# Working the two tiles of a weight group side by side in the feed-forward input phases of a two-layer decoder kernel

## What is computed

```
def swiglu(x, w_in, w_out):
    gate, up = jnp.split(x @ w_in, 2, axis=-1)
    return (jax.nn.silu(gate) * up) @ w_out

h = x + 0.5 * rms_norm(swiglu(rms_norm(x, n_ffn1_pre), ffn1_w_in, ffn1_w_out), n_ffn1_post)
...
h = h + 0.5 * rms_norm(swiglu(rms_norm(h, n_ffn2_pre), ffn2_w_in, ffn2_w_out), n_ffn2_post)
```

## Time and profile before

| | |
|---|---|
| median of 3 runs | 1876.7 us (1876.03 to 1877.76) |
| span of the profiled execution | 1875.0 us, granted TensorE clock 0.993 |
| PE (TensorE matmul) busy | 1816.9 us, 97% |
| PEld (weight load) busy | 1758.3 us, 94% |
| DVE busy | 1342.1 us, 72% |
| ACT busy | 900.3 us, 48% |
| DMA | 368.2 MB, mean 196 GB/s |

### The profile page before, as it was taken

One profiled execution on the slowest core, in us unless ns is written; L12 is line 12 of the kernel. 1 busy time (PEld: TensorE's weight loads), 2 busy tenths in 40 slices (PEclk: granted clock), 3 DMA queues, 4 the chain that ended last, 5 costly groups with the idle time before them and its releaser, 6 DMA issues.

```text
span 1875.0 us, 40290 instructions
## 1 busy us (share of the span) xinstructions
PE 1816.9 (97%) x16206; PEld 1758.3 (94%) x16206; DVE 1342.1 (72%) x2083; ACT 900.3 (48%) x1045; POOL 118.9 (6%) x174
## 2 busy tenths in 40 slices
PE   6999999999999999999999999999999899979998
PEld 6999999988989999999999999998889799979998
DVE  6777577787777868776577766778776776877754
ACT  4443354546564354543354434465567445344433
POOL 0000001111210100000000000010111010000000
PEclk9999999999999999999999999999999999989999
DMA  7776656766764557565667766676777465546654
GB/s 229 207 211 192 178 186 222 239 225 219 270 218 148 188 180 224 160 180 163 182 194 217 204 180 189 201 244 207 231 237 250 160 210 163 177 116 182 182 166 125
DMA packets 433562, 368.20 MB, mean 196 GB/s; under 512 B 9394, under 2 KB 411060, under 8 KB 432754
## 3 DMA queue, kind: packets, MB, share of 16 engines
q1 hardware_dynamic: 409504, 276.60, 49.5%
q0 software_dynamic: 23872, 89.03, 14.1%
HBM read 338.90 MB, written 26.69 MB: 195 GB/s over the span
## 4 chain that ended last, share of the span: by engine, by line
PE 73%; DVE 13%; ACT 6%; issue 5%; DMA 2%; DVEq 0%; SPq 0%; ACTq 0%
PE proj L680 47%; PE proj L703 4%; PE proj L698 4%; PE proj L699 4%; DVE wl L1822 2%; PE proj L654 2%; ACT wh L1331 1%; PE aux L731 1%; PE aux L715 1%; PE aux L1120 1%; PE aux L1067 1%; PE aux L898 1%; DMA raw<-w_mem_v 1%; PE aux L843 1%; PE aux L859 1%
## 5 line engine op out<-in xcount | busy, mean ns | idle before, releaser
L1822 DVE TENSOR_TENSOR wl<-raw,wh 128x2048 fp32r<-128x2048 f32 (+1 forms) x280 | 599.2, 2140 | 199.7 <-ACT wh L1331 175.0
L1331 ACT CAST wh<-raw 128x2048 fp32r<-128x2048 f32 (+1 forms) x280 | 500.2, 1786 | 250.1 <-PE proj L680 106.4
L680 PE MATMUL proj<-xl,wh 128*128 128x264 f32 x2624 | 381.3, 286 | 1.3 <-DVEq L1965 1.3
L680 PE MATMUL proj<-xh,wh 128*128 128x264 f32 x2624 | 380.1, 288 | 0.0
L680 PE MATMUL proj<-xh,wl 128*128 128x264 f32 x2624 | 372.1, 284 | 2.2 <-DVE wl L1822 2.1
L680 PEld LDWEIGHTS proj<-xl,wh 128*128 128x128 f32 x2624 | 342.1, 189 | 14.6 <-issue 12.4
L680 PEld LDWEIGHTS proj<-xh,wl 128*128 128x128 f32 x2624 | 339.5, 189 | 4.0 <-DVE wl L1822 3.9
L680 PEld LDWEIGHTS proj<-xh,wh 128*128 128x128 f32 x2624 | 341.2, 189 | 2.2 <-issue 0.8
L699 PE MATMUL proj<-hl,wh 128*128 128x264 f32 x704 | 173.3, 283 | 0.0
L698 PE MATMUL proj<-hh,wh 128*128 128x264 f32 x704 | 173.0, 283 | 0.0
L1352 ACT ACTIVATE gate<-gate 128x264 f32<-128x264 f32 x88 | 37.4, 425 | 249.1 <-DVEq L1854 249.1
(11 more groups left out here) (465 smaller groups left out, 2283.7 us busy)
## 6 DMA issues: line engine op xcount, KB each, us to landing
raw<-ffn_w_in SPq DMA_DIRECT2D x176, 512.0 KB, 5.2
raw<-w_in SPq DMA_DIRECT2D x80, 1024.0 KB, 5.7
raw<-ffn_w_out SPq DMA_DIRECT2D x64, 704.0 KB, 4.6
sring<-cache_mem_k POOLq DMA_DIRECT2D x32, 512.0 KB, 5.2
sring<-cache_mem_v POOLq DMA_DIRECT2D x32, 512.0 KB, 4.3
out<-sring POOLq DMA_DIRECT2D x32, 512.0 KB, 4.3
sring<-state_gdn POOLq DMA_DIRECT2D x30, 512.0 KB, 5.9
raw<-w_mem_v SPq DMA_DIRECT2D x8, 1024.0 KB, 7.3
```

What stands on the lines that cost most here:

```text
L680: mm = pe.matmul(o, w[:, s, k * 256 + t * P:k * 256 + (t + 1) * P], a[:, k, :], **go)
L1331: act.copy(wh[:, slot, 0:size], raw[:, slot, 0:size]).then_inc(hi_done[slot], 1)
L1822: dve.tensor_sub(wl[:, slot, 0:size], raw[:, slot, 0:size], wh[:, slot, 0:size].bitcast(F32)).then_inc(split_done[slot], 1)
```

## The change

In the 21 groups of each `f1i` and `f2i` phase that are not written by hand, the two tiles are worked together: for each part, for each k-tile, one matmul of t = 0 and then one of t = 1. Both banks are waited for at the head of the group. All groups now have the order HIGH, INPUT_LOW, WEIGHT_LOW. `first_done` is raised by the last matmul but one of the group, `group_done` by the last.

```
-            def products(..., early=None, parts_of=None):
+            def products(..., early=None, parts_of=None, side_by_side=False):
...
+                    elif ph.tiles and side_by_side:
+                        for part in (HIGH, INPUT_LOW, WEIGHT_LOW):
+                            w, a = wl if part == WEIGHT_LOW else wh, low if part == INPUT_LOW else high
+                            if part == WEIGHT_LOW:
+                                pe.wait_ge(split_done[s], n + 2)
+                            for k in range(KT):
+                                for t in range(2):
+                                    bank = 2 * s + t
+                                    if part == HIGH and k == 0:
+                                        pe.wait_ge(bank_free[bank], bank_use(l, ph, i, u, bank) + 1)
+                                    mm = pe.matmul(proj[bank][:, 0:a.shape[2]], w[:, s, k * 256 + t * P:k * 256 + (t + 1) * P], a[:, k, :],
+                                                   start=(part == HIGH and k == 0), stop=(part == WEIGHT_LOW and k == KT - 1))
+                                    if part == WEIGHT_LOW and k == KT - 1:
+                                        mm.then_inc(group_done[s] if t else first_done, 1)
...
-                products(l, "f1i", xh, xl, early=halves(1), parts_of=unscaled(1))
+                products(l, "f1i", xh, xl, early=halves(1), parts_of=unscaled(1), side_by_side=True)
...
-                products(l, "f2i", xh, xl, early=halves(3), parts_of=unscaled(3))
+                products(l, "f2i", xh, xl, early=halves(3), parts_of=unscaled(3), side_by_side=True)
```

More of the change, by code:

```diff
@@ L631, in end, with products @@
                 mm.then_inc(aux_full[PLACE[name][0]], 1)
-            def products(l, name, high, low, kind="", after=None, branch=None, groups=None, mid=None, inner=None, early=None, parts_of=None):
+            def products(l, name, high, low, kind="", after=None, branch=None, groups=None, mid=None, inner=None, early=None, parts_of=None, side_by_side=False):
                 def group(ph, i, u):
```

## The result

The changed kernel takes 1881.69 us (median of 8 runs, 1880.93 to 1885.41) against 1877.23 us (8 runs) for the kernel before: a ratio of 1.0027, with a 95% interval of 1.0019 to 1.0036. It is slower by 4.5 us, and the forecast of 1877.6 us was 4.1 us too low. The profiled execution has a span of 1880.0 us, 5.0 over that of before. Further down, one of the ten runs of `p272_pad` took 9630.85 us where the other nine took 1878.09 to 1882.08; its time and ratio are those of the nine.

What follows compares the result with a forecast made beforehand. The prediction took TensorE's own matmul rate to bound the four input phases. Its terms, 0 + 1.0 - 0.2 + 0 + 0.1 = +0.9 us on 1876.7, gave 1877.6 us, with a range of 1873.5 to 1882.

Steps and rivals of the forecast that it cites:

- What bounds the kernel: Four input phases, 4032 matmuls in 487.6 us: TensorE's own rate sets their time, 120.8 ns per matmul.
- The operands' order: Input phases: new operand order costs 0 to +0.5 ns per matmul; half taken, +1.0 us.
- the operand order costs more: Rival for the input phases: 121.8 ns per matmul, +4.0 us, 1880.6 us in all; chance 0.13.
- The range: Whole kernel: 1873.5 to 1882 us, from pitch -1 to +1 ns per matmul plus smaller terms.
- The banks: Input phases: the 46 more bank changes per group cost or gain 0.
- the rival of a gain of up to 41.7 us: Input phases: alternating banks makes matmuls faster, up to 10.8 ns per bank change, giving 1835 us; chance 0.09.
- The waits for `wl`: Input groups: wait moves to matmul 33, so PE's two hold-ups in the third phase go, -0.2 us.
- The late gate: Input groups: gate and its consumers start about 1.15 us later, hidden by TensorE's work, cost 0.
- The rival of a late cast: Input groups: later loads and cast make PE wait for `wh`, 1881 us; chance 0.08.
- The head of the output phase: Layer 0's fifth output group: later cast makes PE wait 0 to 0.3 us once; +0.1 us taken.
- The sum: Whole kernel: 0 + 1.0 - 0.2 + 0 + 0.1 = +0.9 us, giving 1877.6 us.

Runs made afterwards that it cites:

- p272_pad: Kernel before with input tiles 272 columns apart in memory instead of 264; 1879.95 us, ratio 1.0013.
- e6_inputs_order: Kernel before with each input tile streamed twice in a row and the weight order kept, so wrong products; 1881.66 us, measured once.
- c_before_contig: Kernel before with the eight gate weight tiles contiguous in the slot, then the eight up tiles; 1877.38 us, ratio 1.0000.
- e1_one_bank: Changed kernel's operand order, but 24 matmuls in a row into one bank, sums mixed; 1882.5 us, ratio 1.0032.
- e2_banks_only: Operand order of the kernel before, but a bank change at every matmul, sums mixed; 1877.98 us, ratio 1.0002.
- e10_swept: Changed kernel, but all eight input tiles swept in order twice per part with alternating weight tiles, sums correct; 1876.83 us, ratio 1.0000.
- e4_late_signal: Kernel before with only the first tile's signal moved to the last matmul but one of the group; 1876.93 us, ratio 0.9999.
- e3_pair_apart: Changed kernel's side-by-side order and alternate banks, but each pair's second tile four k-tiles on, sums correct; 1882.38 us, ratio 1.0028.
- e7_one_tile_a: Kernel before, each input phase streaming one input tile throughout (tiles 0 to 3 by phase), wrong products; third phase 120.0 ns, then 121.0 ns per matmul.
- e5_weights_order: Weights in the changed kernel's order, inputs in the order of the kernel before, so wrong products; 1875.29 us, measured once.
- e11_base_16: Kernel before with `xh` moved by 16 bytes, `xl` by 48, what lies behind by 64; 1887.35 us, ratio 1.0055.

## Why the prediction was wrong

**What bounds the kernel** held: TensorE's own pitch sets these phases, before and after.

**The operands' order is the step that failed.** I had bounds of "0 and +0.5 ns per matmul" from the pitch of the output phases, and took half of it, +1.0 us. That the order in which the operands are read sets the pitch was right; the size was wrong, and so was what I read it from. It is (123.27 - 121.80) / 1008 = 1.46 ns, 4032 times, or +5.9 us. An average over the output phases was the wrong bound, because the pitch depends on which tiles follow each other and where they lie, and those phases read other tiles. The rival "the operand order costs more" is what came true; it had a chance of 0.13, with a time of 1880.6 us. I argued against it that the input tiles are read "in the same order as before, each just twice". That was no argument: `e6_inputs_order` has just that difference and the whole loss. Of the two traits that I took over from the output phases, the weight steps of 128 columns don't count (`c_before_contig`), and two matmuls in a row with one weight tile weren't tested. The rival's 121.8 ns was also an end of a rounding: the runs of eleven take 1.34 and 1.33 us by turns, 121.4 ns in the mean. The neighbour of the row:

```profile
191.44 1.33 PE proj L703 x11
```

**The range.** The time lies 0.3 us inside its upper end of 1882, and that is luck. The range was made with +1 ns per matmul at most, and the pitch rose by 1.46; the terms as measured would give 1876.7 + 5.5 = 1882.2 us.

**The banks** at 0 held (`e1_one_bank`, `e2_banks_only`), and the rival of a gain of up to 41.7 us fell. The 10.8 ns over the 110.0 ns of 264 columns are not the price of adding into the same bank. The Trainium skill, "TensorE: Matmul & The Clock Gate", section "Back-to-back issue gap", gives N / 2.4 + 2.5 ns as the isolated gap of a single matmul, without a budget for weight loads; at 264 columns that is 112.5 ns, an estimate by that page's formula; the rows here show 120.0 to 123.3 with a weight load before each matmul. What the rest is was not measured.

**The waits for `wl`** went, as said: the third phase is at 123.27 like the others, and at 121.80 in `e10_swept`. Over all four that is 487.6 - 4 x 121.80 = 0.4 us, where I took 0.2 from the two rows. These waits aren't in every kernel with the early wait: `c_before_contig` waits for `wl` as early as the kernel before does, and all its phases took 121.80 us.

**The late gate** cost 0, as said. The rival of a late cast fell: `e4_late_signal` has the same lateness and no loss.

**The head of the output phase** cost nothing that the rows show, where I took 0.1 us. In the changed kernel the fifth group's cast is this row, and the low-part piece ahead of that group the one below it:

```profile
195.93 1.38 ACT L1345 CAST wh<-raw 128x1408 fp32r<-128x1408 f32 x1 [3.66 <-DMA raw<-ffn_w_out]
```

```profile
196.70 1.34 PE proj L717 x11
```

The cast ends at 197.31 and PE needs it at 198.04: 0.7 us left of the 0.9 of before. The runs of eleven that start at 188.69 and 236.73 us in the same chain are 48.04 us apart for 12 groups, as before.

**The sum** by the measured terms is +5.9 - 0.4 = +5.5 us for the four phases. The spans of the two profiled executions differ by 5.0, the medians by 4.5. The gap of 0.5 to 1.0 us to the sum wasn't traced; the eight runs of one kernel lie 4.5 to 5.1 us apart.

## What to carry to other kernels

In a phase where TensorE is never held up, a new order of the same matmuls gains nothing through waits, and can lose through the pitch. So bound the pitch by the full spread that the rows show for that shape, not by an average of another phase. To test such a reordering, change one stream at a time (banks, weights, inputs), even if the products then pair tiles that don't belong together: pieces of some 1000 matmuls in the chain tell 0.01 ns per matmul, far below what total times resolve. If tiles must be worked side by side, sweeping the input tiles in the old order with alternating weight tiles costs nothing here.

## What the runs showed of the hardware

- For matmuls of 128x128 by 264 columns in fp32r, each with its weight load and at the granted clock of 1.00, the time from start to start depends on the places and the order of the input (moving) tiles. It is 120.0 to 123.3 ns for one tile repeated, 120.8 for the eight tiles in steps of 1 or 3, 121.6 for steps of 7, 122.3 for steps of 5 and for each tile twice, 122.1 when every second tile is four on (`e3_pair_apart`), 121.7 with tiles 1088 in place of 1056 bytes apart, and 122.8 with the tensors moved by 16 and 48 bytes.
- It isn't set by place and order alone. In the third phases of `p272_pad` and `e7_one_tile_a` another pitch follows a short wait: 120.8 in place of 121.6 ns, and 121.0 in place of 120.0. In the kernel before the pitch is 120.8 after the same waits, too (152 matmuls in 18.36 us from 1073.96 on).
- It doesn't depend on the order of the weight tiles or on their steps of 128 or 256 columns, nor on whether the bank changes at every matmul or every 24.
- Where PE waits for nothing, it repeats: in the changed kernel, `e1_one_bank`, `e5_weights_order`, `e6_inputs_order`, `c_before_contig`, `e10_swept` and `e11_base_16` the four phases agree to 0.01 us in 122 to 124 us, while DVE, ACT and the DMAs do different work beside them.
- Open: why one place or order is better than another, and what a wait changes in it. Neither the place within some block of bytes nor the step from the end of a tile to the next start orders the numbers; no run looked into what stands behind them.
